# Expert rows through DRAM, packed weights and a fourth split buffer in a two-layer mixer and MoE kernel

## The reference

```
def moe_swiglu(h, w_router, w1, w3, w2):
    logits = (h @ w_router).astype(jnp.float32)
    top_v, top_i = lax.top_k(logits, TOP_K)            # TOP_K = 2, 8 experts, width 3584
    gates = jax.nn.softmax(top_v, axis=-1)
    combine = jnp.sum(jax.nn.one_hot(top_i, N_EXPERTS, dtype=jnp.float32) * gates[..., None], axis=-2)
    out = jnp.zeros_like(h)
    for e in range(N_EXPERTS):
        out = out + combine[..., e:e + 1].astype(h.dtype) * swiglu(h, w1[e], w3[e], w2[e])
    return out
```

## Time and profile before

| | |
|---|---|
| median of 3 executions | 1763.06 us (1761.28 to 1763.15) |
| profiled execution | 1761.89 us, span 1760.0 us, mean granted TensorE clock 0.974 |
| TensorE busy | 1648.2 us (94%) |
| VectorE busy | 1336.6 us (76%) |
| ScalarE busy | 1059.4 us (60%) |
| Pool busy | 112.1 us (6%) |
| DMA | 427.99 MB, 243 GB/s over the span |
| chain that ended last | TensorE 74%, VectorE 11%, ScalarE 5%, issue 5%, DMA 4% |

### The profile page before, as it was taken

The page is one execution under the profiler, slowest core; times in us unless marked ns, Lnnn a source line. Parts: engine busy times, 40 slices in busy tenths (PEclk is TensorE's granted clock), DMA queues, the critical chain, the costliest instruction groups (busy, mean ns, idle before and its releaser), DMA issues.

```text
span 1760.0 us, 27088 instructions
## 1 busy us (share of the span) xinstructions
PE 1648.2 (94%) x9618; PEld 1418.2 (81%) x9618; DVE 1336.6 (76%) x1250; ACT 1059.4 (60%) x1039; POOL 112.1 (6%) x151
## 2 busy tenths in 40 slices
PE   6888969999797897799999999999999999999997
PEld 5877859999797786688888888888888888888886
DVE  4888555444458865788888888888888888888885
ACT  4634454433353335477677677677777777676775
POOL 1142100000005210000000000000000000000000
PEclk8999989999899999799999999999999999999999
DMA  7520036452352103499999999999999999999993
GB/s 230 159 72 25 16 120 216 165 192 95 119 168 71 42 1 118 143 356 363 311 366 351 321 368 358 323 366 356 325 366 338 340 367 327 352 366 328 347 367 114
DMA packets 327137, 427.99 MB, mean 243 GB/s; under 512 B 6849, under 2 KB 294753, under 8 KB 326961
## 3 DMA queue, kind: packets, MB, share of 16 engines
q1 hardware_dynamic: 326304, 425.28, 71.8%
q0 software_dynamic: 640, 2.00, 0.4%
q10 hardware_dynamic: 144, 0.05, 0.0%
HBM read 426.25 MB, written 1.05 MB: 243 GB/s over the span
## 4 chain that ended last, share of the span: by engine, by line
PE 74%; DVE 11%; ACT 5%; issue 5%; DMA 4%; SPq 0%; DVEq 0%; ACTq 0%; POOL 0%; POOLq 0%
PE bank L375 29%; PE bank L400 15%; PE bank L1121 8%; PE bank L378 7%; PE bank L628 6%; PE bank L403 4%; DMA ring<-in_moe_w 3%; ACT wh L435 2%; DVE wl L439 2%; PE bank L660 1%; PE bank L388 1%; PE bank L1126 1%; DVE ml L615 1%; DVE hs L1877 1%; DVE rw L1779 1%
## 5 line engine op out<-in xcount | busy, mean ns | idle before, releaser
L439 DVE TENSOR_TENSOR wl<-ring,wh 128x2048 fp32r<-128x2048 f32 x369 | 844.6, 2293 | 211.4 <-ACT wh L435 198.8
L435 ACT ACTIVATE wh<-ring 128x2048 fp32r<-128x2048 f32 x369 | 705.9, 1915 | 130.2 <-PE bank L400 43.5
L375 PE MATMUL bank<-wh,xh 128*128 128x512 f32 x896 | 361.7, 404 | 0.9 <-DVE xl L868 0.9
L375 PE MATMUL bank<-wh,xl 128*128 128x512 f32 x896 | 351.1, 392 | 0.0
L375 PE MATMUL bank<-wl,xh 128*128 128x512 f32 x896 | 349.6, 390 | 0.0
L375 PEld LDWEIGHTS bank<-wh,xh 128*128 128x128 f32 x896 | 168.4, 188 | 37.5 <-issue 4.9
L375 PEld LDWEIGHTS bank<-wh,xl 128*128 128x128 f32 x896 | 168.3, 188 | 37.3
L375 PEld LDWEIGHTS bank<-wl,xh 128*128 128x128 f32 x896 | 169.0, 189 | 32.0
L400 PE MATMUL bank<-wh,gh 128*128 128x512 f32 x448 | 175.5, 392 | 3.5 <-DVE gl L525 3.4
L400 PE MATMUL bank<-wh,gl 128*128 128x512 f32 x448 | 174.6, 390 | 0.0
L400 PE MATMUL bank<-wl,gh 128*128 128x512 f32 x448 | 174.6, 390 | 0.0
(11 more groups left out here) (294 smaller groups left out, 2564.3 us busy)
## 6 DMA issues: line engine op xcount, KB each, us to landing
ring<-in_moe_w SPq DMA_DIRECT2D x336, 1024.0 KB, 8.3
ring<-in_ffn_w SPq DMA_DIRECT2D x33, 1024.0 KB, 6.1
ring<-in_w_in SPq DMA_DIRECT2D x24, 1024.0 KB, 5.3
ring<-in_w_out SPq DMA_DIRECT2D x8, 1024.0 KB, 5.1
ring<-in_w_in SPq DMA_DIRECT2D x2, 640.0 KB, 4.0
const<-in_const SPq DMA_DIRECT2D x1, 1200.0 KB, 14.4
proj<-in_x SPq DMA_DIRECT2D x4, 256.0 KB, 6.7
out<-wide SPq DMA_DIRECT2D x1, 1024.0 KB, 4.0
```

The lines of the kernel that those rows point to most:

```text
L375: ins = nc.tensor.matmul(up_bank(run, par, 0)[:], x[:, 0:C], w[b][:, k], **kw)
L435: nc.scalar.activation(o, src[0], ACT.Copy).then_inc(sem("w_high"), 1)
L439: nc.vector.tensor_tensor(split(wl[:, buf]), src[0], split(wh[:, buf]).bitcast(F32), ALU.subtract).then_inc(sem("w_split"), 1)
```

## The change

- **Rows through DRAM.** New DRAM tensors `job_x` and `job_y`, 2048 rows of 4 KB each. Both are filled with zeros by two Pool DMAs in layer 0. Pool scatters the token rows into `job_x` with four indirect DMAs once the slots are known. For jobs 1 and on, Pool loads 128 rows into `xrow`, and `gather` becomes eight transposes of them; only job 0 still gathers with `sel`, now built by VectorE.
- **Results through DRAM.** `yj` is stored to `job_y` by Pool. After the last job four indirect DMAs fetch, for each token, its two result rows into `ring`; VectorE multiplies them by the gates and adds them to the residual, which has been turned to token order (`xtok`, sixteen more transposes and four copies ahead of job 0). The final norm is done per token. `scatter`, `scattered`, the gate matrices, `turn_gates`, `compare_slots` and the two closing sets of transposes and norm sums are gone.
- **No zeroing.** The first `pe_down` of a job starts its banks, behind a wait for `acc_copied`.
- **Packed weights.** The host lays each 1 MB load out as 128 rows of 8 KB, for the mixer, the dense part and the experts.
- **A fourth buffer** of `wh` and `wl`, used by stage up(0,0) of each job after the first. ScalarE and VectorE split it ahead of `act_end_a` and `dve_end_a`, so ahead of down(13) and of gh and gl of pair 12. TensorE's order stays down(13), up(0,0).

```
-        wh = sb("wh", [P, 3, 8 * T], F32R)
-        wl = sb("wl", [P, 3, 8 * T], F32R)
+        wh = sb("wh", [P, 4, 8 * T], F32R)
+        wl = sb("wl", [P, 4, 8 * T], F32R)
...
             def up(self, m, part):
                 if isinstance(m, int) and m == 0:
+                    if self.follows and part == 0:
+                        return self.stages - 1, 3
                     return self.stages + part, part
```

TensorE, the border:

```
             with pe.Fori(1, n_jobs) as j:
-                run, nxt = job(j - 1), job(j)
+                run, nxt = job(j - 1), job(j, True)
                 pe_turn_gated(pe, run, last)
                 gather(j)
-                turn_gates(j - 1)
-                pe_down(pe, run, last, True)
+                pe_down(pe, run, last, True, followed=True)
+                pe.wait_ge(sem("x_split"), x_before(1, 2) + 2 * j + 1)
+                pe_up(pe, nxt, 0, 0, 0)
                 pe.wait_ge(sem("x_split"), x_before(1, 2) + 2 * j + 2)
-                pe_up(pe, nxt, 0, 0, 0)
                 pe_up(pe, nxt, 0, 0, 1)
-                scatter(j - 1)
-                pe.wait_ge(sem("scatter_added"), 4 * (j - 1) + 2)
-                zero_acc((2, 3))
-                pe_steps(pe, nxt)
+                pe_steps(pe, nxt, j)
```

the new gather:

```
+                pe.wait_ge(sem("x_loaded"), 16 * j)
+                for half in range(2):
+                    for d in range(4):
+                        k = 4 * half + d
+                        turn(bank[5 + half][:, d * C:(d + 1) * C], xrow[:, k * P:(k + 1) * P],
+                             sig="gathered" if d == 3 else None)
```

ScalarE, the border:

```
-                act_end_a(act, run)
                 up(0, 0, 0, 0)
+                act_end_a(act, run, True)
                 act_gated_high(act, run, last)
                 gathered(j)
                 up(0, 0, 0, 1)
-                gates(j - 1)
+                up(1, 0, 1, 0)
                 acc(j - 1)
-                up(1, 0, 1, 0)
                 act_start(act, nxt)
```

VectorE, the border:

```
-                dve_end_a(dve, run)
                 up(0, 0, 0, 0)
+                dve_end_a(dve, run, True)
                 dve_gated_low(dve, run, last)
                 gathered(j)
                 up(0, 0, 0, 1)
                 up(1, 0, 1, 0)
                 up(1, 0, 1, 1)
                 dve_gate(dve, nxt, 0, 0)
-                scattered(j - 1)
                 down(0, 0, 0)
-                compare_slots(j + 1)
                 dve_steps(dve, nxt)
```

Pool:

```
+            def load(j):
+                pool.dma_start(xrow[:], job_x[bass.ds(j * C, C), :]).then_inc(sem("x_loaded"), 16)
+
+            def store(j, sig="y_stored"):
+                pool.wait_ge(sem("acc_copied"), 2 * j + 2)
+                pool.dma_start(job_y[bass.ds(j * C, C), :], yj[:]).then_inc(sem(sig), 16)
...
             with pool.Fori(1, n_jobs) as j:
-                job_matrices(j)
+                pool.wait_ge(sem("gathered"), 2 * j)
+                load(j)
+                store(j - 1)
+            j = last_job(pool)
+            store(j, "last_stored")
+            pool.wait_ge(sem("last_stored"), 16)
+            for tt in range(TT):
+                for i in range(2):
+                    pool.indirect_dma_start(yrow(tt, i), None, job_y,
+                                            bass.IndirectOffsetOnAxis(ap=sidx[:, 2 * tt + i:2 * tt + i + 1], axis=0)
+                                            ).then_inc(sem(f"y_rows{tt}"), 16)
```

SP:

```
-                        load(slot, slot_of(slot), w[bass.ds(row13, D), bass.ds(m * T, T)].rearrange("(k p) n -> p k n", p=P))
+                        load(slot, flat_slot(slot), w[bass.ds(row + m * P, P), :])
...
-                down(1, 1, True, 0)
+                down(1, 1, True, 1)
```

Pool, layer 0, behind the last hgrn level:

```
+                if layer == 0:
+                    settle(nc.gpsimd.memset(xrow[:], 0.0))
+                    for rows_, sig in ((job_x, "zero_filled"), (job_y, "y_stored")):
+                        pool.dma_start(rows_.rearrange("(j p) d -> p j d", p=C),
+                                       xrow[:].unsqueeze(1).broadcast_to([P, MAXJOBS, D])).then_inc(sem(sig), 16)
```

More of the change, by code:

```diff
@@ L320, in program, with __init__ @@
         class Run:
-            def __init__(self, pairs, moe, stages, items, before_pairs, loads):
+            def __init__(self, pairs, moe, stages, items, before_pairs, loads, follows=False):
                 self.pairs, self.moe = pairs, moe
@@ L389, in pe_turn_gated, with pe_down @@
                 ins.then_inc(sem("g_turned"), 1)
-        def pe_down(pe, run, m, last=False):
-            stage, buf = run.down(m, last)
+        def pe_down(pe, run, m, last=False, first=False, followed=False):
+            stage, buf = run.down(m, last, followed)
             pe.wait_ge(sem("w_split"), stage + 1)
@@ L415, in step @@
                 pe_up(pe, run, m, par, 1)
-                pe_down(pe, run, m - 1)
+                if first:
+                    wait(pe, "acc_copied", 2 * j)
+                pe_down(pe, run, m - 1, first=first)
             n = run.pairs - 1
+            if run.moe:
+                step(1, 1, True)
+                with pe.Fori(0, n // 2) as i:
+                    step(2 * i + 2, 0)
+                    step(2 * i + 3, 1)
+                return
             with pe.Fori(0, n // 2) as i:
@@ L723, in gather @@
                                tt == 0, tt == 1, "gathered" if d == 3 and tt else None)
[L725 to L738, removed]
+            def gather(j):
+                pe.wait_ge(sem("x_loaded"), 16 * j)
[4 more added lines that the diff above has]
+                             sig="gathered" if d == 3 else None)
             last = PAIRS_E - 1
-            gather(0)
-            zero_acc((2, 3))
+            gather_first()
             run = job(0)
+            pe.wait_ge(sem("xm_copied"), 4)
             pe.wait_ge(sem("x_split"), x_before(1, 2) + 2)
@@ L1518, in _ @@
             pe_moe(pe, mm, turn)
-            norm(2 * DEPTH)
-            for k in range(KT):
-                pe.wait_ge(sem("hT_ready"), 2 * DEPTH * KT + k + 1)
-                for tt in range(TT):
-                    turn(bank[k // 2][:, tt * T + k % 2 * P:tt * T + (k % 2 + 1) * P], hT[:, k, tt * P:(tt + 1) * P],
-                         sig="out_turned" if k % 2 and tt else None)
         @block.scalar
@@ L1759, in _ @@
                     act_ffn_dense(act)
-            act_moe(act, copy, f, square)
-            root(2 * DEPTH)
-            for b in range(4):
-                act.wait_ge(sem("out_turned"), b + 1)
-                copy(wide[:].rearrange("p (a b) t -> p a (b t)", a=TT)[:, :, b * T:(b + 1) * T],
-                     bank[b][:].rearrange("p (a t) -> p a t", a=TT), "out_ready")
+            act_moe(act, copy, f)
         @block.vector
@@ L2088 @@
     arrays = {f"in_{n}": np.ascontiguousarray(inputs[n]) for n in NAMES}
+    arrays.update((f"in_{n}", a) for n, a in weights(inputs).items())
     arrays["in_const"] = constants()
```

229 lines of the change are left out of this document (127 added, 102 removed).

## The result

| | before | after |
|---|---|---|
| median | 1762.17 us (1761.06 to 1763.15) | 1781.11 us (1775.71 to 1783.75) |
| profiled execution, its span | 1761.89, 1760.0 us | 1780.91, 1779.3 us |
| mean granted clock | 0.974 | 0.959 |
| TensorE busy | 1648.2 us | 1611.2 us |
| copy of `yj` to copy of `yj`, jobs 1 to 6 | 126.3 to 127.6 us | 129.1 to 129.6 us |

The ratio of the times is 1.010, with a 95% interval of 1.0077 to 1.0123: the changed kernel is slower by 1%, 18.9 us against a forecast of 14.2. TensorE has 37 us less to do and the kernel takes 19 us more.

What follows compares the result with a forecast made beforehand. TensorE was taken to bound the MoE stage (busy 126.3 of 126.6 us a job). Borders -15.4, clock +17.5, second stall +11.1, head -0.8, tail +1.8 gave +14.2 on 1761.9: 1776 us, range 1742 to 1788.

Steps and rivals of the forecast that it cites:

- case A: Whole kernel: first stall, low clock and second stall all come, 1776 us (1768 to 1788); chance 0.42.
- first stall: At each job border TensorE waits 5.0 us ahead of down(12), as gh and gl queue behind late loads.
- half clock: Behind each border's stall TensorE runs at 1.2 GHz for a while, losing 2.5 us per border, 17.5 in all.
- second stall: Ahead of the next job's up(2,0), weights share engines with Pool's transfers: 1.7 us at six borders, 0.9 last, 11.1 total.
- the tail: After the last job: y store, indirect reads, adds and per-token norm replace scatter and norm sums, +1.8 us.
- the head: Before and in job 0: the slot compare that holds gl back goes, -0.8 us.
- C: Rival at the borders: clock stays at 2.4 GHz through the 5 us stall, 1758.6 us, or 1747 with B's condition; chance 0.15.
- B: Rival: as A, but Pool's megabyte falls into a gap of the ring, so no second stall, 1765 us; chance 0.18.
- What goes from the border: Per border: gather, gates' turn, scatter and zeroing go, -8.4 us; turns add 0.9, the gl wait 0.3.
- E: Rival in layer 0: the zero fills block Pool until one has drained, +10 us, 1786 us; chance 0.10.
- D: Rival at the borders: both loads land by 1474.2, down(12) is never late, kernel at 1712 to 1724 us; chance 0.12.
- F: Rival on loads: the 358 GB/s limit holds, first stall grows 1.1 us at seven borders, 1784 us; chance 0.03.

Runs made afterwards that it cites:

- experiment 4: Changed kernel with Pool loading the x rows a job ahead and storing the y rows only after eighteen stages of the next job: 1764.14 us.
- experiment 1: Changed kernel with the old split order (gh, gl and down(13) ahead of the next job's first up stage) and three buffers: 1727.47 us.
- Experiment 3: Changed kernel with SP issuing both loads for the next job's first up stages ahead of down(13)'s load: 1736.46 us.
- Experiment 2: Changed kernel with five useless matmuls of constants on TensorE ahead of down(12) in every job: 1771.88 us.
- experiment 7: Changed kernel with early issue of the next job's first up loads and Pool's transfers moved, fourth buffer and its order kept: 1723.64 us.
- experiment 8: Changed kernel with old split order, three buffers, Pool's transfers moved, and VectorE's pair 13 gl and half of x ahead of the next up split: 1721.22 us.
- experiment 6: The old-order, three-buffer kernel of experiment 1 with weight packing taken away, rows of 1 KB and 4 KB again: 1753.74 us.

## Why the prediction was right, and where it was not

The forecast was case A, 1776 us, and the mechanism is A's: first stall, half clock, second stall. That the sum came within 5.1 us isn't luck in its large terms, which were each near what they measured; the tail, the head and the time that the loads take together were off. By its terms:

- **First stall.** Forecast 5.0 us at each border, measured 4.58 to 5.56, mean 5.2. Its parts: the string from landing to matmul was put at 4.7 us and is 1489.3 to 1493.97. The load move was taken as 2.55 us per MB; loads in a row land 2.47 us apart (424 GB/s in the stall), inside the bounds and nearer the lower one. Yet the three loads take 9.6 to 10.6 us from the first issue to the last landing where the sum had 2.1 + 3 x 2.55 = 9.8. At the sixth border the second one is issued 1.57 us behind the first (1480.25) and lands 3.2 us behind it; in experiment 4 three issued within 1 us land 2.48 us apart. The same sum gives 11.1 us for the kernel before, where the earlier trace rows show 11.8, so this could have been seen. (The sum's own 1484.0 less 1478.9 is 5.1, not 5.0.) Experiments 1 and 3 take the stall away by the two ends of its cause, order and load.
- **The clock.** Forecast 2.5 us per border from the earlier trace rows, measured 16.6 in all, 2.4 each. Experiment 2 brings it back with the stall in place, and the stretches at 0.50 end C.
- **Second stall.** Forecast 11.1 us, one wait of 1.7 us ahead of up'(2,0) at six borders and 0.9 at the last; measured 10.5, in two waits of about 1.0 and 0.55 us at six borders and one of 1.00 at the last. Experiment 4 removes it. It is not Pool's alone: experiment 1 keeps Pool's transfers and has 4.0 us. The store of y lands in 8.6 us and the load of x in 11.4 beside the ring; so the megabyte isn't hidden, and B falls.
- **What goes from the border.** 8.4 us were taken out per border and 1.2 put in for turns and gl. The eight turns and the wait behind them take 1.17 us (1499.55 to 1500.72). A job of experiment 7 is 118.2 us without these turns and its 1.26 us wait (1.5 with the 0.26 of experiment 4), one of experiment 8 worked out the same way 118.6, where the sum had 118. So the border gave 8.0 to 8.4 us.
- **Head.** Forecast -0.8, measured -1.6: down(0) of job 0 starts at 741.69 instead of 743.27. 0.9 of it is the wait of the earlier trace rows, gone as forecast; 0.7 is that the first up matmul of the expert stage is at 730.33 instead of 731.00, which the sum put at nothing. The scatters into `job_x`, about 1 us of issue each, lie before it.
- **Fills.** Hidden, as forecast, which ends E. Pool's timeline against the 10.95 us of the earlier trace rows:

```profile
126.81 0.95 POOL L1132 MEMSET xrow<- 128x1024 f32 x1
128.06 1.23 POOL L1134 DMA_DIRECT2D job_x<-xrow  x1 [0.30 <-POOL xrow L1132]
129.29 1.16 POOL L1134 DMA_DIRECT2D job_y<-xrow  x1
137.65 3.09 POOL L1143 TENSOR_TENSOR mtm<-rw,const 128x512 f32<-128x512 f32 x2 [7.19 <-DVE rw L1796]
```

The second fill needs 46.3 us to land, but Pool goes on after 1.2 us of issue and still has 7.19 us idle.

- **Tail: the term that was mis-sized.** Forecast +1.8, measured +4.2 (24.2 against 20.0 us). The chain of waits there, answering to the earlier trace rows:

```profile
1756.35 0.86 issue
1757.21 0.54 POOL job_y L957
1757.75 2.38 issue
1760.13 1.23 POOLq L148
...
1762.96 0.94 POOL ring L971
1763.90 0.30 issue
1764.21 6.11 DMA ring<-job_y,sidx
```

The store lands 2.9 us after its issue began, less than the 4.0 taken. The indirect reads are what the sum got wrong: it had 3.0 us to landing and 1.3 for each one more, but they are issued 1.3 us apart (0.94 to 1.01 and 0.30) and land 4.5, 5.4, 5.6 and 6.1 us later. The fourth is in at 1770.32, 14.1 us after the copies of `yj` end (1756.22, from the chain), where the sum had 4.0 + 3.0 + 4 x 1.3 = 12.2. That is 1.9 of the 2.4 us missed. (The recorded 5.4 us for the first two reads is 3.0 + 2 x 1.3 = 5.6, and its last terms add to 1761.2, not 1761.4; the two slips cancel.)

Added up as the profile prints them, 36.5 + 16.6 + 11.1 - 7 x (8.4 - 1.17) - 1.6 + 4.2 make 16.2 of the 19.3 us between the spans. What is missing is mostly what a wait costs beyond its printed idle time: 22 waits at some 0.26 us are 5.7 us. Against it stand waits for gl of 0.60, 0.23 and 0.72 us at other borders of the kernel before, which are gone and which the sum, with 0.15 for each border, left out. With both the list comes to 20.4, about 1 us too much.

**The rival on the other side (D)** did not come: the loads land at 1489.3, not early enough by five us. Experiment 3 is its condition, built, and gives 1736.5 us, where D had 1712 to 1724. D does not name the second stall, which stays until Pool's transfers are moved (experiment 7, 1723.6 us), and has nothing for VectorE, where with the weights in time three splits in a row still hold gl back by 1.26 us.

**The limit of 358 GB/s (F).** The stretch in the stall moves 424 GB/s, and 1 MB loads land 2.47 us apart. The Trainium skill (DMA: Bandwidth & Descriptors, "Where 436 GB/s comes from") says that HBM to SBUF is bound at about 358 GB/s; the trace of this one core disagrees by 18%, and the measurement decides. By this figure of the Trainium skill the first stall would have been 6.1 us, an estimate. The Trainium skill's rule (DMA: Bandwidth & Descriptors, "Queues, rings and completion order") that an engine takes turns between queues with work fits the 3.5 against 11.4 us of experiment 4.

## What to carry to other kernels

A buffer more is not worth anything if the wait that fills it stands ahead of work that is needed sooner: ask of each in-order engine what is queued behind the new wait, and when its consumer starts. A removal at the border of a loop is only worth what the next late thing leaves, so move the loads together with the removal (experiments 3 and 7). Waits shorter than the tail of a modelled matmul are not printed at all: compare the distance of like matmuls between two kernels (8.43 against 8.59 us a pair in experiment 6). And a wait on TensorE of 5 us costs the wait and half of the low-clock stretch after it, here 7.6 us for 5.2.

## What the runs showed of the hardware

- Loads of 1 MB in rows of 8 KB land 2.47 us apart when they are issued together, 424 GB/s in the DMA engines, with one core at work; in rows of 1 KB it was 347.
- Not every stall of a size brings the clock down. In experiment 6 it fell to 0.50 after waits of 2.35, 2.73, 3.19 and 2.06 us and not after 2.98, 2.49 and 2.01 us; in experiment 1 not after 2.18. The 5 us stalls of the changed kernel all brought it down.
- Half a megabyte through Pool's queue takes 2.9 us (store) and 3.5 us (load) alone, and 8.6 and 11.4 beside the ring's loads.
- Indirect reads of 128 rows of 4 KB take 0.94 to 1.01 us to issue with 0.30 between them, and 4.5 to 6.1 us to land.
